# A two-layer hybrid decoder step on Trainium2: ScalarE takes a convolution tap, gate products go to four array quadrants, and two queues are dealt out anew

## What is computed

```python
x = x + 0.5 * _swiglu(_rmsnorm(x, lp['norm_ffn1']), ...)
proj = (_rmsnorm(x, lp['norm_mix']) @ lp['w_in']).astype(F32)
p_rw, p_rg, p_gdn, p_gla = jnp.split(proj, IN_SPLITS, axis=-1)
# RWKV-7, RG-LRU, gated delta net, gated linear attention
mixed = jnp.concatenate([o_rw, o_rg, o_gdn, o_gla], axis=-1)
x = x + mixed @ lp['w_out']
x = x + 0.5 * _swiglu(_rmsnorm(x, lp['norm_ffn2']), ...)
```

## Time and profile before

| | |
|---|---|
| median of 3 runs | 1360.48 us (1359.74 to 1360.81) |
| the profiled execution, its own time | 1361.45 us |
| its span in the profile | 1359.7 us |
| TensorE busy | 1334.3 us, 98% |
| VectorE busy | 856.3 us, 63% |
| ScalarE busy | 695.2 us, 51% |
| mean granted TensorE clock | 0.998 |

### The profile page before, as it was taken

One profiled execution on the slowest core, in us unless ns is written; L12 is line 12 of the kernel. 1 busy time (PEld: TensorE's weight loads), 2 busy tenths in 40 slices (PEclk: granted clock), 3 DMA queues, 4 the chain that ended last, 5 costly groups with the idle time before them and its releaser, 6 DMA issues.

```text
span 1359.7 us, 31412 instructions
## 1 busy us (share of the span) xinstructions
PE 1334.3 (98%) x12576; PEld 1294.5 (95%) x12576; DVE 856.3 (63%) x1327; ACT 695.2 (51%) x1003; POOL 72.5 (5%) x113
## 2 busy tenths in 40 slices
PE   7999999999999999999999999999999999999997
PEld 7999999998888999999999999999988899999997
DVE  6656533897876766653376655349988767556433
ACT  7554423856565654443364454247466655444423
POOL 0000000200030100000010000011001210000001
PEclk9999999999999999999999999999999999999999
DMA  8544454322313644444454454443223244444441
GB/s 297 173 144 152 143 154 153 109 79 79 111 50 110 202 152 143 151 155 153 142 189 152 154 151 146 151 140 109 82 76 96 65 157 155 153 143 150 152 144 53
DMA packets 50768, 185.90 MB, mean 137 GB/s; under 512 B 5760, under 2 KB 6272, under 8 KB 50176
## 3 DMA queue, kind: packets, MB, share of 16 engines
q1 hardware_dynamic: 49104, 177.37, 41.1%
q10 hardware_dynamic: 1584, 7.35, 1.5%
HBM read 180.14 MB, written 4.56 MB: 136 GB/s over the span
## 4 chain that ended last, share of the span: by engine, by line
PE 85%; DVE 10%; ACT 2%; issue 2%; DMA 0%; POOL 0%; DVEq 0%; ACTq 0%; POOLq 0%
PE ps L478 26%; PE ps L480 26%; PE ps L479 26%; DVE wl L1581 2%; DVE ar L1738 2%; PE ps L844 1%; PE ps L747 1%; DVE ar L1652 1%; PE ps L1030 0%; PE ps L815 0%; DVE ar L1729 0%; ACT ar L1289 0%; PE ps L1008 0%; DVE raw L1956 0%; PE ps L888 0%
## 5 line engine op out<-in xcount | busy, mean ns | idle before, releaser
L478 PE MATMUL ps<-xh,wh 128*128 128x320 f32 x1952 | 612.5, 314 | 10.2 <-DVE xl L1603 7.9
L1581 DVE TENSOR_TENSOR wl<-raw,wh 128x1024 fp32r<-128x1024 f32 x332 | 407.7, 1229 | 317.9 <-ACT wh L1181 317.6
L480 PE MATMUL ps<-xh,wl 128*128 128x320 f32 x1952 | 604.5, 310 | 0.0
L479 PE MATMUL ps<-xl,wh 128*128 128x320 f32 x1952 | 604.5, 310 | 0.0
L1181 ACT ACTIVATE wh<-raw 128x1024 fp32r<-128x1024 f32 x332 | 349.3, 1054 | 357.9 <-PE ps L480 341.0
L478 PEld LDWEIGHTS ps<-xh,wh 128*128 128x128 f32 x1952 | 367.8, 188 | 20.9 <-issue 7.6
L479 PEld LDWEIGHTS ps<-xl,wh 128*128 128x128 f32 x1952 | 367.9, 188 | 0.6
L480 PEld LDWEIGHTS ps<-xh,wl 128*128 128x128 f32 x1952 | 367.8, 188 | 0.0
L478 PE MATMUL ps<-hid_h,wh 128*128 (+1 forms) x704 | 217.5, 309 | 0.0
L479 PE MATMUL ps<-hid_l,wh 128*128 (+1 forms) x704 | 217.5, 309 | 0.0
L480 PE MATMUL ps<-hid_h,wl 128*128 (+1 forms) x704 | 217.5, 309 | 0.0
(11 more groups left out here) (289 smaller groups left out, 941.9 us busy)
## 6 DMA issues: line engine op xcount, KB each, us to landing
raw<-wts SPq DMA_DIRECT2D x332, 512.0 KB, 3.5
ms<-mst ACTq DMA_DIRECT2D x2, 1440.0 KB, 8.2
mout<-ms ACTq DMA_DIRECT2D x2, 1440.0 KB, 6.7
x<-xT SPq DMA_DIRECT2D x4, 320.0 KB, 5.1
yT<-x SPq DMA_DIRECT2D x4, 320.0 KB, 2.4
cs<-cst SPq DMA_DIRECT2D x1, 652.0 KB, 8.4
pr<-par ACTq DMA_DIRECT2D x1, 429.0 KB, 4.5
pr<-par ACTq DMA_DIRECT2D x1, 425.0 KB, 5.2
```

Of the source, the lines that this page charges most:

```text
L478: pe.matmul(out, a, rh, start=start, stop=False)
L479: pe.matmul(out, a, rl, start=False, stop=False)
L480: return pe.matmul(out, b, rh, start=False, stop=stop)
L1581: tt(wl[:, s, :], raw_of(layer, n), wh[:, s, :].bitcast(F32), ALU.subtract).then_inc(lo_ready.sem, 1)
```

## The change

1. Tap 0 of each `gdn_conv(j)` goes to ScalarE, as a copy with a scale per channel (`first_tap(j)`); VectorE's `gdn_conv(j)` waits for it and does taps 1 to 3.
2. The four products of an RG-LRU gate go to four quadrants of the array instead of two: channel half b of pair p writes half `b ^ p` of the PSUM bank. ScalarE's `rg_sigmoid` reads pair 1 in two pieces, since its halves are swapped.
3. The lists of calls of VectorE and ScalarE are put in another order.

TensorE's list is the same. The first two parts:

```diff
                 else:
-                    on(pe, layer, "rg_gates", 2)
+                    on(pe, layer, "rg_gates", 3)
                 for p in range(2):
                     for b in range(2):
-                        ins = pe.matmul(ps[half[b], 6 + p, 0:TOK], wrg[g][half[b], p, :], xc[half[b], p, :], ...)
+                        ins = pe.matmul(ps[half[b ^ p], 6 + p, 0:TOK], wrg[g][half[b], p, :], xc[half[b], p, :], ...)
...
+                def first_tap(j):
+                    on(act, layer, "shift_kept")
+                    on(act, layer, in_read, T_GDN + j + 1)
+                    say(act.activation(cv[:, j, 0:CVP - 3], gcp[:, j, 0:CVP - 3], ACT.Copy, scale=P("gcw", j)), "tap0")
...
                     for p in range(2):
-                        say(act.activation(dst[:, p, :], ps[:, 6 + p, 0:TOK], ACT.Tanh, scale=0.5, ...), "rg_gates")
+                        for to, at in pieces(p):
+                            say(act.activation(dst[to, p, :], ps[at, 6 + p, 0:TOK], ACT.Tanh, scale=0.5, ...), "rg_gates")
...
                 def gdn_conv(j):
                     on(ve, layer, "shift_kept")
-                    for k in range(CONV):
+                    on(ve, layer, "tap0", j + 1)
+                    for k in range(1, CONV):
```

More of the change, by code:

```diff
@@ L1364, in _ @@
                 ahead(1)
+                ahead(2)
                 act.wait_ge(S["xm"].sem, S["xm"].upto(layer, 1))
@@ L1388, in _ @@
                 st(act.activation(Pinv[:], cum[:], ACT.Exp, scale=WDEC))
+                on(act, layer, "lora_mm", 3)
+                for p in range(2):
+                    say(act.activation(rw_g[:, p, :], ps[:, 2 + p, 0:TOK], ACT.Copy), "rw_gc")
                 act.wait_ge(S["prev"].sem, S["prev"].upto(layer))
@@ L1399, in _ @@
                 st(act.activation(tiny[:, 11:13], tiny[:, 11:13], ACT.Exp, scale=-1.0))
-                on(act, layer, "lora_mm", 3)
-                for p in range(2):
-                    say(act.activation(rw_g[:, p, :], ps[:, 2 + p, 0:TOK], ACT.Copy), "rw_gc")
+                ahead(6)
+                ahead(7)
+                ahead(8)
                 act.wait_ge(S["gla_ab"].sem, S["gla_ab"].upto(layer))
@@ L1408, in _ @@
                 say(act.activation(ltm, ltm, ACT.Ln, bias=C("one")), "gla_ln")
-                ahead(8)
                 ahead(9)
-                ahead(10)
                 eye(0)
-                on(act, layer, "rw_rows_mm", 1)
-                home(rVt, 2, "rw_rows")
                 on(act, layer, "rw_rows_mm", 2)
@@ L1418, in _ @@
                 home(bLt, 6, "rw_rows")
+                on(act, layer, "rw_rows_mm", 1)
+                home(rVt, 2, "rw_rows")
+                first_tap(0)
+                ahead(10)
+                inverse_t(0, 1)
+                first_tap(1)
+                across(0, 1)
+                ahead(11)
+                across(0, 2)
                 act.wait_ge(S["Gb_mm"].sem, S["Gb_mm"].upto(layer))
@@ L1449, in _ @@
                 across(0, 4)
+                ahead(15)
                 act.preload_act_table_set("exp_and_others")
+                inverse_t(0, 4)
+                gla_scale(1)
                 eye(1)
-                ahead(16)
-                inverse_t(0, 4)
                 on(act, layer, "gc_kept")
@@ L1466, in _ @@
                 home(bvt, 4, "gdn_rows")
+                ahead(19)
+                inverse_t(1, 2)
+                across(1, 2)
                 ahead(20)
@@ L1491, in _ @@
                 say(act.activation(lB, lB, ACT.Exp, scale=1.0 / GLA_TAU), "leB")
+                ahead(23)
+                ahead(24)
+                act.wait_ge(S["rg_y"].sem, S["rg_y"].upto(layer))
+                on(act, layer, "rgc_kept")
+                st(act.activation(rgt[:], rr[:], ACT.Tanh, scale=4.0))
                 inverse_t(1, 5)
-                ahead(24)
                 on(act, layer, "gla_rows_mm")
@@ L1531, in _ @@
                 log_of(1, 1)
+                m_evac(3)
                 root_of(1, 1)
@@ L2086, in _ @@
                 evac(5)
+                ahead(3)
+                rw_mix(0, 2)
                 ahead(4)
-                rw_mix(0, 2)
+                evac(6)
                 ahead(5)
-                evac(6)
+                gla_floor()
                 rw_scaled()
+                evac(7)
+                rw_rest()
                 ahead(6)
-                evac(7)
-                gla_floor()
-                rw_rest()
+                ahead(7)
                 evac(8)
-                ahead(7)
                 rw_mix(4, 6)
+                gdn_gate()
                 ahead(8)
-                gdn_gate()
                 rw_masks()
+                evac(9)
                 ahead(9)
-                evac(9)
+                gla_decay()
                 evac(10)
-                ahead(10)
                 inverse(0, 0)
@@ L2108, in _ @@
                 gdn_conv(0)
+                ahead(10)
+                rw_gain()
+                gla_diff(1)
                 gdn_conv(1)
-                gla_decay()
                 evac(11)
-                rw_gain()
+                inverse(0, 1)
                 ahead(11)
                 evac(12)
-                inverse(0, 1)
+                evac(13)
                 ahead(12)
-                evac(13)
                 gdn_conv(2)
-                ahead(13)
                 gdn_conv(3)
+                evac(14)
+                gdn_conv(4)
                 inverse(0, 2)
                 gdn_decays()
-                evac(14)
-                gdn_conv(4)
                 gdn_conv(5)
-                gla_diff(1)
+                evac(15)
+                ahead(13)
                 gdn_bounds()
-                evac(15)
+                inverse(0, 3)
+                ahead(14)
                 evac(16)
-                ahead(14)
-                inverse(0, 3)
                 ahead(15)
@@ L2182, in _ @@
                 take(6)
-                rg_steps()
                 g_r(0)
-                ahead(24)
+                ahead(23)
                 g_u(0)
+                rg_root(0)
                 g_m(0)
                 gla_chain()
+                centering()
                 g_r(1)
-                rg_root(0)
                 rg_root(1)
@@ L2198, in _ @@
                 g_r(2)
-                ahead(25)
                 g_u(2)
-                rg_enter()
+                rw_shift()
                 dec_add(0)
@@ L2215, in _ @@
                 o_low(2, rr[:], 1)
-                rw_shift()
+                ahead(24)
                 gated(0)
@@ L2222, in _ @@
                 finish(2)
+                o_low(6, yo[2][:], 4)
+                ahead(25)
                 dec_add(4)
-                o_low(6, yo[2][:], 4)
                 for k in range(KT - 1):
```

124 lines of the change are left out of this document (56 added, 68 removed).

## The result

The changed kernel took 1365.76 us in the median of 6 executions (1364.65 to 1366.28), the kernel before 1360.64 on the same chip (1359.32 to 1361.41). The ratio is 1.003, with a 95% interval of 1.002 to 1.0041; the medians are 5.1 us apart. The prediction was 1357.1, its range ended at 1360.2, and "slower" had a chance of 0.05. So the sign is wrong, and the miss is 8.7 us.

What follows compares the result with a forecast made beforehand. TensorE, busy 1334.3 of 1359.7 us, was taken to bound the kernel. From 1361.45 us, -2.8 for both layers (-1.40 each) and -1.5 for the clock drop gave 1357.15, stated as 1357.1; range 1353.0 to 1360.2.

Steps and rivals of the forecast that it cites:

- step 7: Gates to recurrences: gates save 0.90 us a layer; no further wait, least margin 0.5 us at take(4) behind rg_steps.
- slower rival: Taps and tile 19's split come late through ScalarE; beyond about 2.2 us late a layer the change loses; chance 0.05.
- F: Old stall: tile 17 waits for evac(15), 0.95 us a layer; forecast to go.
- G: Old stall: gdn_beta waits for the exponential L1448, about 0.9 us a layer; forecast to stay.
- C: New stall: rw_rows waits for rw_masks, forecast at +0.77 us a layer.
- D: Old stall: the first inverse_t waits for home, 0.37 us a layer; forecast to grow by 0.47.
- rivals with one drop and two drops: Low clock stays: one drop 1358.6 us, chance 0.20; drops in both layers, or G later, 1360.1, chance 0.10.
- A: Old stall: tile 9 waits for evac(7), 0.38 us a layer; forecast to go.
- B: Old stall: rw_products waits for rw_rest, 0.39 us a layer; forecast to go.
- E: Old stall: inverse_y(1,2) waits for across(1,2), 0.55 us a layer; forecast to go.
- H: New stall: tile 23 waits for evac(21), forecast at +0.68 us a layer.
- rival in which the new waits don't form at all: C, D and H vanish: 1352.6 us; half of it 1354.8; chance 0.20 for half formed or less.

Runs made afterwards that it cites:

- e2: The changed kernel with one wait added on GpSimd, so that decay(1) waits for take(4): 1360.56 us, ratio to before 0.9998.
- e12: The kernel before run once more, unchanged, one execution for its profile: 1363.9 us.
- e6: The changed kernel with GpSimd's decay(1) held back as in e2 and the gates' products in two quadrants as before: 1364.96 us.
- e5: The kernel before with two parts of the change, first taps on ScalarE and gates in four quadrants: 1359.70 us.
- e4: The kernel before with only the first taps of the six GDN tiles put on ScalarE: 1359.12 us, ratio 0.9985.
- e7: The changed kernel with decay(1) held back as in e2 and the first taps on VectorE again: 1363.40 us, ratio 1.0012.
- e9: The changed kernel with e2's wait and, on VectorE, rw_masks, evac(21), inverse(0,0) and gdn_bounds moved earlier: 1352.79 us, ratio to before 0.994.
- e1: The changed kernel with rg_steps back behind take(4), evac(25) and gla_reads(6), and ScalarE's tanh behind inverse_t(1,5): 1370.41 us, ratio 1.0065.

## Why the prediction was wrong

**The step that failed** is step 7: "From here to the recurrences I find no wait; the least margin is 0.5 us, at `take(4)` behind `rg_steps`." I had priced `rg_steps` from its rows in the old place: 0.82 and 0.68 for the body. In the new place L1924 started beside GpSimd's L2304 and took 1.07, and the two TENSOR_SCALAR met `decay(1)` and took 2.27. A margin of 0.5 became a wait of 1.8 us. e2 shows the cause, and that it was worth 5.2 us with the clock behind it. The margin itself was not there either: without `decay(1)` e2 still waits 0.16, with the 0.25 that L1924 lost in it. The prediction named the spot ("if a new wait sits at tile 19 or behind `take(4)`"), but gave it no price and no chance; its slower rival was built on the taps and tile 19, where nothing happened.

**The second step** that failed: "The clock drop behind F and G should go, as F is gone: -1.5." F went, and C and D took its place ahead of G. e2, which has no stall at `take(4)`, has the drop in both layers. So the term was about +1.5 against that profile of before, where I had -1.5. The rivals with one drop and two drops had this right; 1360.1, given for two, is close to what e2 measured (1360.6). It is also why that number is no more than the time before: the kernel before has one or two drops itself. How many there are varies from execution to execution; the changed kernel's own profile has one. That C and D bring the drop is a tendency by the count under e12 (10 of 12 layers) and was not shown by a run of its own.

**The rest of the sum**, by e2. Its way to L867 without the drop (5.00 us at tile 18 instead of 3.48, so 1.52) is 133.47 - 1.52 = 131.95. The kernel before has 133.13 without one. That is -1.18 a layer, where steps 1 to 7 had 0.47 - 0.95 + 0.13 - 0.90 = -1.25. This is layer 0; e2's layer 1 is 0.57 longer, by a pause of 0.52 at `inverse_y` that no other profile has at that length. By terms:

- Steps 1 and 2 (A, B against C): A and B went; C is 1.0 shown, 1.08 with what lies under the tail, against 0.77. Forecast 0, measured +0.3.
- D: from 0.37 to 0.82, forecast +0.47. Right.
- F: gone, -0.95. Right.
- G: 0.9 forecast, 0.7 measured. -0.2 instead of 0.
- E gone, H 0.75 instead of 0.68. Right.
- Gates: -0.90 forecast, -1.06 in e6 against e2 and -0.73 in e5 against e4, where 0.21 went to the wait for the tanh. Right. The rival of quadrants without overlap is out.
- `m_evac(2)`: its wait is 0.4 as before; the 0.15 did not come.
- The list of stalls left out two more in the recurrences, L1017 for `g_m` (0.54) and the second wait of L865 (0.19). No kernel here removes them, so the sum does not feel it, but 3.9 a layer was not all.
- Taps: "Neither enters the sum by itself". In the new order as it was built VectorE's saving is spent on what was put in its place; yet by e7's waits the new order would lose 3.2 us without it (the medians say 2.8, not clear of noise), and e4 shows that alone it gains 2.2.

Added up from the forecast of 1357.1: two drops instead of none, +3.0, and 0.2 a layer for C, G, H, gates and `m_evac(2)`, +0.4, make e2's 1360.6; the stall at `take(4)` and the clock behind it, +5.2, make the measured 1365.8.

The rival in which the new waits don't form at all is what e9 came to build: 1352.8, and the estimate had been 1352.6. That it is so close is partly luck: the estimate kept G, which e9 has lost, and had neither its wait at tile 13 nor its gap of 1.1.

## What to carry to other kernels

An instruction that is moved keeps its duration only if its neighbours on the other engines stay the same: before you price a move on VectorE, look at what GpSimd does at the new place, and look for rows of one shape with two durations, since 0.28 and 1.04 us for the same product is the price list. Where two engines collided here, delaying the one with slack by one wait (e2) was better than another order (e1). And when short pauses turn the clock down in some executions only, price a term by its stretch in the trace and not by the median, and expect a removed pause to help with the clock only if no other takes its place.
